# Gated linear attention with its state kept in PSUM, g in seven products, and the decays of q and k on GpSimd

## The reference

```python
S_t = diag(a_t) S_{t-1} + k_t^T v_t ;  o_t = q_t S_t        # 4 heads, dk 128, dv 256
y_a = rms_norm_heads(o, gn_w) * silu(g)
p   = causal_multiscale_pool(u) ; y_b = (p @ pool_w + pool_b) * pool_scale * silu(z)
merged = sigmoid(gate_a) * (y_a @ w_a) + sigmoid(gate_b) * (y_b @ w_b)
out = layer_norm(ALPHA * x + merged @ w_o)
```

## Time and profile before

| what | us |
|---|---|
| median of 3 runs | 585.56 (585.38 to 586.18) |
| the profiled execution | 584.62 |
| span of its slowest core | 583.1 |
| PE busy | 566.3 (97% of the span) |
| DVE busy | 441.9 (76%) |
| ACT busy | 290.4 (50%) |
| POOL busy | 113.4 (19%) |

### The profile page before, as it was taken

How to read it: one execution, slowest core, us unless ns; L and a number is a source line. 1 busy time by engine, 2 the same in 40 slices (tenths; PEclk the granted TensorE clock), 3 DMA queues, 4 the chain that set the end, 5 groups by cost and what they waited for, 6 DMA issues and landing times.

```text
span 583.1 us, 10349 instructions; the slowest of 8 cores (581.2 to 583.1 us)
## 1 busy us (share of the span) xinstructions
PE 566.3 (97%) x2990; PEld 279.7 (48%) x2990; DVE 441.9 (76%) x841; ACT 290.4 (50%) x619; POOL 113.4 (19%) x184
## 2 busy tenths in 40 slices
PE   6899999999999999999999999999999999999993
PEld 2344445555555655444444444444444455555562
DVE  2478988888777797887877888466785577788786
ACT  2479965666666676454232333657633244322223
...
DMA packets 48008, 60.21 MB, mean 103 GB/s; under 512 B 30864, under 2 KB 36624, under 8 KB 45648
## 3 DMA queue, kind: packets, MB, share of 16 engines
...
...
## 4 chain that ended last, share of the span: by engine, by line
PE 91%; DVE 3%; DMA 2%; issue 1%; SPq 1%; ACT 1%; POOL 1%; DVEq 0%; ACTq 0%; POOLq 0%
PE pb L951 27%; PE pb L1045 14%; PE pb L679 9%; PE pb L1628 8%; PE pb L712 8%; PE pb L409 5%; PE pb L1513 4%; PE pb L429 4%; PE pb L1553 2%; PE pb L1499 2%; DMA A<-head 2%; PE pb L764 1%; PE pb L769 1%; PE pb L781 1%; SPq L306 1%
## 5 line engine op out<-in xcount | busy, mean ns | idle before, releaser
L1045 PE MATMUL pb<-A,ws 128*128 128x512 bf16 x256 | 64.1, 379 | 0.0
L679 PE MATMUL pb<-A,xT 128*128 128x512 bf16 x256 | 62.4, 379 | 0.2 <-ACT A L673 0.2
L951 PE MATMUL pb<-A,ws 128*128 128x512 bf16 x216 | 53.1, 379 | 0.0
L956 ACT COPY sgm_t<-pb 128x512 f32<-128x512 f32 x54 | 31.7, 586 | 27.2 <-PE pb L951 26.4
L1646 ACT ACTIVATE wg_s<-xT 128x512 bf16<-128x512 f32 (+1 forms) x32 | 19.9, 623 | 49.0 <-DVE xT L1637 48.6
L951 PE MATMUL pb<-xT,ws 128*128 128x512 bf16 x172 | 44.2, 379 | 0.0
L804 POOL TENSOR_SCALAR A<-A,eblast 128x256 bf16<-128x256 f32 x30 | 29.7, 990 | 66.3 <-ACT A L805 39.3
L1666 POOL TENSOR_SCALAR small<-small 128x1 f32<-128x1 f32 x15 | 19.3, 1285 | 119.8 <-DVE small L1661 119.8
L1045 PEld LDWEIGHTS pb<-A,ws 128*128 128x128 bf16 x256 | 25.0, 98 | 30.2
L1022 ACT ACTIVATE sgm_t<-sgm_t 128x512 f32<-128x512 f32 x24 | 15.1, 630 | 48.0 <-DVE sgm_t L982 24.8
L259 POOL DMA_DIRECT2D ws<-wts x10 | 5.5, 548 | 168.6 <-PE pb L951 82.7
...
## 6 DMA issues: line engine op xcount, KB each, us to landing
ws<-wts POOLq DMA_DIRECT2D x10, 1024.0 KB, 10.7
...
A<-wts POOLq DMA_DIRECT2D x7, 1024.0 KB, 26.7
...
```

Of the source, the lines that this page charges most:

```text
L679: PE(lambda e, k=k: e.matmul(pb[bank][:, :], xTc(c, k), W.ap[:, k, :], start=(k == 0), stop=(k == KC - 1)), r=[W.b], w=[bb[bank]])
L951: PE(lambda e, k=k: e.matmul(pb[bank][:, :], u(k), x(k), start=first and k == 0, stop=k == 3, skip_group_check=True), r=[ub] + xb, w=[bb[b ...
L956: ACT(lambda e: e.copy(SG[s], pb[bank][:, :]), r=[bb[bank]], w=[b_SG[s]])
L1045: PE(lambda e, k=k: e.matmul(pb[bank][:, :], W.ap[:, k, m * 128:(m + 1) * 128], aT[:, k, tb * 512:(tb + 1) * 512], start=(k == 0), stop=(k ...
```

## The change: what it does, and the diff

- The scan of the gate restarts every 256 tokens instead of every 128, so q and k of a pair of chunks share one origin, and the state needs a decay once for each pair.
- The state is summed in PSUM: bank 6 for hp 0, bank 7 for hp 1. After the odd chunk of a pair DVE scales the bank in place. The bf16 copy of both heads is one instruction, on DVE after even chunks and on ACT after odd ones. The decayed copies on ACT and POOL and the DVE updates go.
- g of pairs 1 to 7 is done in seven products too, in banks 3, 2 and 4; v and g take turns, and all seven v products and the first of g stand in two steps. GV sums for g are made on DVE in steps 0 to 2.
- 20 of the 24 decays of q and k of blocks 1 to 3 move from DVE to POOL, one in each of the steps 2 to 17, two each in steps 0 and 1. One of the five x sums of each pair from the second on goes to POOL.
- The first part of the merged weights (`wp_part`) moves from steps 25 to 27 into steps 27 and 28, with other banks; the first `direct_u` starts at (28, 1). u0 is loaded at step 12 into the room of the first block of q and k.

```diff
-        POOL(lambda e: e.memset(mask_t[:].rearrange("p (c t) -> p c t", c=4)[:, :, 0:1], 0.0), w=[b_ones])
+        POOL(lambda e: e.memset(mask_t[:].rearrange("p (c t) -> p c t", c=2)[:, :, 0:1], 0.0), w=[b_ones])
...
-        fin_pending += [(tb, h) for tb in range(1, 4) for h in range(4)]
+        fin_pending += [(1, h) for h in range(FIN_D)]
...
-        kd = [R1f[:, 0:1024], R1f[:, 1024:2048]]
+        kd = [A4[:, 0:1024], A4[:, 1024:2048]]
...
-            UENG(lambda e: e.tensor_tensor(GU[i], a, b, op), w=[b_GU[i]])
+            (POOL if pair > 1 and i in (3,) else DVE)(lambda e: e.tensor_tensor(GU[i], a, b, op), w=[b_GU[i]])
...
-            bB, bA, bD = (2, 7)[kind], 3, 4
+            bB, bA, bD = ((2, 3, 4), (3, 2, 4))[kind]
...
-                ACT(lambda e: e.copy(pb[bA][:, :], pb[bB][:, :]), r=[bb[bB]], w=[bb[bA]])
+                dup = lambda: ACT(lambda e: e.copy(pb[bA][:, :], pb[bB][:, :]), r=[bb[bB]], w=[bb[bA]])
+                opened[kind] = pair >= GQ0
+                if opened[1 - kind] and pair >= GQ0:
+                    dups[1 - kind].append(dup)
+                else:
+                    dup()
             elif i in (2, 0):
+                while g_wait:
+                    g_wait.pop(0)()
...
-                    vg_evac(1, c, blk, GT[t], [b_GT[t]])
+                    g_wait.append(lambda: vg_evac(1, c, blk, GT[t], [b_GT[t]]))
...
-                    pb[6][:, j * 256:(j + 1) * 256], k_t, vj,
-                    start=True, stop=True), r=[k_b, vB], w=[bb[6]])
+                    pb[6 + hp][:, j * 256:(j + 1) * 256], k_t, vj,
+                    start=(c == 0 and j == 0), stop=True, skip_group_check=True), r=[k_b, vB], w=[bb[6 + hp]])
...
+            S, sB = pb[6 + hp], bb[6 + hp]
+            if c % 2:
+                for j in range(2):
+                    h = hp * 2 + j
+                    DVE(lambda e, j=j, h=h: e.tensor_scalar(
+                        S[:, j * 256:(j + 1) * 256], S[:, j * 256:(j + 1) * 256], eblast[:, c // 2, h:h + 1], None, ALU.mult),
+                        r=[b_eblast[c // 4 * 4 + h]], w=[sB])
+
+        def st_copy(n):
...
+            if S_ENG[c % 2]:
+                DVE(lambda e: e.tensor_copy(o, S[:, :]), r=[sB], w=[oB])
+            else:
+                ACT(lambda e: e.copy(o, S[:, :]), r=[sB], w=[oB])
...
-            bks = (0, 1) * 4 if blk else (7, 4, 3, 4, 7, 4, 7, 4)
+            bks = (0, 1) * 4 if blk else (2, 2, 3, 4, 2, 3, 0, 4)
...
-                if blk or k % 2 == 0 or k > 4:
+                if blk or k not in (2, 7):
...
+        ORDER = ((5,), (2, 0, 6), (1,), (3, 4, 15), (), (10, 16, 12), (11,), (13, 14))
+        GV_AT = [[(0, 0), (0, 1)], [(0, 1), (1, 0)], [(1, 0), (1, 1)], [(1, 1)], [(2, 0), (2, 1)]]
...
+            if pair >= GQ0:
+                for j, units in enumerate(ORDER):
+                    for u in units:
+                        put(n + j // 2, j % 2, gq, u // 10, pair, u % 10)
...
-        for n, pos, f, args in ((25, 1, wp_part, (0, 0, 1)), (26, 0, wp_part, (0, 1, 2)), (26, 1, wp_part, (0, 2, 4)),
-                                (27, 0, wp_part, (0, 4, 6)), (27, 1, wp_part, (0, 6, 8)), (28, 0, direct_u, (0, 0)), (28, 1, direct_u, (0, 1)),
...
+        for n, pos, f, args in ((27, 0, wp_part, (0, 0, 1)), (27, 1, wp_part, (0, 1, 3)), (28, 0, wp_part, (0, 3, 7)),
+                                (28, 0, flush_g, ()), (28, 1, wp_part, (0, 7, 8)), (28, 1, direct_u, (0, 0)),
...
+        FIN_AT = {0: (4, 5), 1: (6, 7)}
+        FIN_AT.update({n: (n + 6,) for n in range(2, 18)})
...
             st_sq(n)
+            st_copy(n)
+            for i in FIN_AT.get(n, ()):
+                finalize_one(1 + i // 8, i % 8 // 2, (i % 2,), POOL)
...
-            if n // 4 + 2 < NT // 2:
-                for u in {1: (2, 0), 2: (6, 3), 3: (4,)}.get(n % 4, ()):
+            if n % 4 == 3 and n // 4 + 2 < NT // 2:
+                for u in (2, 0, 3, 6, 4):
                     gu_sum(u, n // 4 + 2)
+            if n == 12:
+                ld(wu[0], "u0", extra=lastops([b[0] for b in b_qbb + b_kbb]))
```

More of the change, by code:

```diff
@@ L653, in build_program @@
             "p (j f) -> p j f", j=2) for s in range(2)] for hp in range(2)]
-        S_f = [A4[:, TB + 4096 + hp * 1024:TB + 4096 + (hp + 1) * 1024].bitcast(F32).rearrange(
-            "p (j f) -> p j f", j=2) for hp in range(2)]
         junk = [A4[:, TB + 7168 + i * 256:TB + 7168 + (i + 1) * 256] for i in range(4)]
@@ L663, in build_program @@
         b_Sbf = [[Buf() for _ in range(2)] for _ in range(2)]
-        b_S = [Buf() for _ in range(2)]
         b_ss = [Buf() for _ in range(2)]
@@ L672, in vg_evac @@
             o, oB = vg_seg(kind, c, blk), b_vg[kind][c % 4][blk]
+            if not kind and (c % 2, blk) in V_DVE:
+                DVE(lambda e: e.tensor_copy(o, src), r=sB, w=[oB], extra=vg_free(kind, c, blk))
+                return
             ACT(lambda e: e.activation(o, src, AF.Silu if kind else AF.Copy), r=sB, w=[oB],
@@ L754, in kd_block @@
                    r=[b_kbb[h][0], b_ident], w=[bb[bank]])
-            DVE(lambda e: e.tensor_copy(kd[i], pbT[bank][:, 0:1024]), r=[bb[bank]], w=[b_kds[i]])
+            DVE(lambda e: e.tensor_copy(kd[i], pbT[bank][:, 0:1024]), r=[bb[bank]], w=[b_kds[i]], extra=lastops(b_la))
         def st_UO1(n):
@@ L787, in st_state @@
             c, hp = n // 2, n % 2
[L788 removed]
             if c == NT - 1:
                 return
[L791 to L806 removed]
+            S, sB = pb[6 + hp], bb[6 + hp]
[6 more added lines that the diff above has]
+        def st_copy(n):
+            c, hp = n // 2, n % 2
+            if c == NT - 1:
+                return
+            S, sB = pb[6 + hp], bb[6 + hp]
+            o, oB = Sbf_s[hp][(c + 1) % 2].rearrange("p j f -> p (j f)"), b_Sbf[hp][(c + 1) % 2]
+            if S_ENG[c % 2]:
+                DVE(lambda e: e.tensor_copy(o, S[:, :]), r=[sB], w=[oB])
+            else:
+                ACT(lambda e: e.copy(o, S[:, :]), r=[sB], w=[oB])
         def st_sq(n):
@@ L1253, in build_program @@
             if n == 19:
-                ld(wu[1], "u1", extra=lastops(b_kT[0:8]))
+                ld(wu[1], "u1", extra=lastops(b_kT[0:8] + b_kds))
             if n == 28:
                 POOL(lambda e: e.memset(mask_t[:], 1.0), w=[b_ones], extra=[P.last["pe"]])
-            if n in (26, 27):
-                for b in b_V[1][n % 2 * 2:n % 2 * 2 + 2]:
-                    b.r = [P.last["pe"]]
+            if n in (27, 28):
+                for i in {27: (0, 1, 3), 28: (2,)}[n]:
+                    b_V[1][i].r = [P.last["pe"]]
             on_dve(tail_ops.get(n, ()))
```

79 lines of the change are left out of this document (40 added, 39 removed).

## The result

| | before | after |
|---|---|---|
| median (4 runs each, side by side) | 585.47 (585.15 to 586.18) | 590.0 (588.82 to 591.58) |
| profiled execution, span of its slowest core | 584.62, 583.1 | 591.58, 590.0 |
| spans of the eight cores | 581.2 to 583.1 | 584.0 to 590.0 |
| PE, DVE, ACT, POOL busy | 566.3, 441.9, 290.4, 113.4 | 565.6, 442.5, 294.4, 116.7 |
| PE instructions | 2990 | 2962 |

The ratio is 1.0077, with a 95% interval of 1.0052 to 1.0103: slower, as forecast. PE issues the 28 matmuls less and is busy only 0.7 us less: it waits.

What follows compares the result with a forecast made beforehand. PE was taken as the bound, busy 15.99 of 15.99 us a pair. Terms -6.04 + 5.4 + 1.75 + 1.7 = +2.8 gave 587.4 to 588.4, stated as 588.0 us; own range 586.8 to 590.5, whole range 581.5 to 591.5.

Steps and rivals of the forecast that it cites:

- Matmuls saved, 6.04: g of seven pairs falls from 32 matmuls to 28, taking 6.04 us off PE, the only gain.
- Pairs 2 to 7, 0.90 of waits each: PE waits for ACT copies: v0 0.62, v1 0.07, g0 0.21; 0.90 a pair, 5.4 us in six pairs.
- The sign that I gave for being right: Pairs of 16.0 to 16.3 us, each with a wait of about 0.6 for the dup; ACT above 80%.
- Pair 1, 1.75: In pair 1 g0 waits for the negation in DVE's queue; 1.75 us with small waits, bounds 0.2 to 3.5.
- I therefore add nothing: DVE's sums with two SBUF inputs lose little beside POOL's operations (0.62 instead of 0.41), so no time was added.
- The end, 1.7: End of the loop: `wp_part` pieces, O1 of step 28 and first `direct_u` wait 1.96, less 0.24: 1.7 us.
- POOL's product, 1.9: A 128x512 product on POOL takes 1.9 us, twice POOL's 0.93 row; POOL has 13.3 of 15 us and hides.
- Edits at nothing: Scan mask, smaller exponent, state's first matmul start, u0 at step 12, k's transposed copies, kd's new place: no cost.
- the upper bound of a pair's waits (1.3): Pairs 2 to 7: 1.3 us of waits a pair if DVE's x sums come after the dup.
- Sum: Whole kernel: -6.04 + 5.4 + 1.75 + 1.7 = +2.8 us, forecast 588.0.
- Rival 1: Pairs 2 to 7: the dup reaches v0 in time, ACT's waits stay small; 581 us, chance 0.30.
- Rival 3: POOL's decays hold DVE's GV or x sums: 1.9 more in pair 1, 0.5 a pair in 2 to 5; 591.9, chance 0.07.

Runs made afterwards that it cites:

- the first experiment: Against the changed kernel: pair 1's g direct, seven products of g from pair 2 on, GV sums spread over steps 1 to 5; 587.98 us, 1.0053.
- the last experiment: Against the changed kernel: g's products from pair 2, GV sums moved, v5, x sum 2 and g1's SiLU earlier, g2 ahead of g0; 584.58 us, 0.9998.

## Why the prediction was right, point by point

- **Matmuls saved, 6.04.** Right: 28 fewer.
- **Pairs 2 to 7, 0.90 of waits each.** Measured 0.69 (4.2 in six pairs, not 5.4): about 0.2 too much, and the main wait was misplaced. I let v0 wait 0.62 for the dup, with DVE's x sums behind it only as an upper bound. In the trace v2 waits 0.44 for the x sum first, and the dup (2.93 behind g4 where I had 3.10, so 0.45 of its own against PE's 2.48) is covered by it. g0 0.20 and v1 0.06 are as predicted (0.21, 0.07). Pairs became 0.16 shorter, where I had 0.04 longer. The sign that I gave for being right, a pair of 16.0 to 16.3 with a wait of 0.6 for the dup and ACT above 80%, did not come: 15.84, a wait of 0.44 for DVE, ACT at 69%.
- **Pair 1, 1.75.** The step that failed. The order of DVE's queue was right (g0 was late for the negation; taking it out took the wait out), but "I therefore add nothing" for POOL beside DVE was wrong: 0.88 for late outputs and 2.21 for g0, 3.1 in all. (The sum itself gives 10.35 - 8.52 = 1.83, not 1.75; that matters little.) DVE's rows above show where most of the 1.35 us over my 1.75 went. From mask to outputs 0.85 passes where I had 0.34, since the norm is late beside DVE's sums: 0.5. The last half sum holds the queue for 1.11 where I had 0.61, since POOL's decay is in its way: 0.5; moving the decays away gave 0.3 of it back. The two half sums beside the norm take 1.40 instead of 1.22: 0.2. The row that I took for evidence (a sum of 0.62 beside a POOL operation) had POOL reading one input of half the columns, and that sum ended before POOL did. The Trainium skill, SBUF — State Buffer, "Who interferes with whom", whose rule I judged not borne out in its whole length, says that a DVE instruction with two SBUF inputs contends with a POOL instruction that reads SBUF, and that the ports which the two share are an exclusive lock; the half sum of the first experiment agrees (1.43 us, ending 0.56 behind POOL).
- **The clock.** Not in any case of mine: 1.7 us on five of eight cores, behind pair 1's wait. It is the difference between +1.7 in the loop and +3.4.
- **The end, 1.7.** Right in place, a little too dear: waits of 0.57, 0.81 and 0.33 (1.7; I had 1.96), less 0.41 of before where I took off 0.24, so 1.3. (The 0.24 was read off busy time, which shows such a wait 0.16 too short.)
- **POOL's product, 1.9.** It takes 1.15 us, where DVE has 0.42. The Trainium skill, GPSIMD Engine Reference, section 3.1, whose figure is for an addition of fp32 numbers, led to an estimate of 1.1, closer than my doubling of the earlier trace rows.
- **Edits at nothing.** The scale in place takes 1.08 for two, where I took 0.475 each; no wait names it, but it stands in the queue of 3.5 us that makes v2's sum late, and whether it has a part there stays open: on ACT it left v2 waiting 0.42, with the squares late instead. The new place of all x sums in one step was in my sum only as the upper bound of a pair's waits (1.3); in the control without g's products it and POOL's part in it cost 0.9 to 1.3 a pair.
- **Sum.** +2.8 predicted, +1.7 in the loop on quiet cores, +3.4 with the clock, +4.5 in the medians. On core 1 the waits add up: -6.05 for the matmuls, +3.1 in pair 1, +4.2 in pairs 2 to 7, +1.7 at the end, less three waits of the kernel before (0.39, 0.41 and the 0.42 behind the loop). That the total lay near the forecast is in part luck: pairs 1.2 too dear and pair 1 1.35 too cheap cancel, and the 1.7 of the clock was in no term. With the 0.42 that the end point of the loop hides, 3.9 of the 4.5 are accounted for on the five slower cores; the last 0.6 stay open. The cores lie 6 us apart after the change and 1.9 before; in the profiled execution core 0, the slowest, also lost 3.4 us ahead of the loop, in waits of 2.5 for the conversion of x (line 312), which the change does not touch, and in a fall of the clock behind them (0.70 from 40 to 44).

Rival 1 (waits vanish) fell at once, since a pair takes 15.84 and not 15.1 to 15.4; its best form, the last experiment, shows that the pair can run at 15.55, not at 15.1. Rival 3's mechanism was real, in pair 1 and at 1.2 instead of 1.9.
